# Sparse, dilated and windowed attention in one layer: choices of key blocks eight tiles apart, and the compression units' finishing cut in three

## The chip, the core and the metric

The kernel runs on one core of a Trainium2 chip. The engines are TensorE (PE for matmuls, PEld for weight loads), VectorE (DVE), ScalarE (ACT), GpSimd (POOL) and SyncE (SP, which issues transfers). The metric is the device time of one launch in microseconds (us); lower is better. Rows of the profile write L12 for line 12 of the kernel before.

## The reference, cut to what matters

One transformer layer over 2048 tokens of width 1024: a norm and an input projection, a mix of three attentions, an output projection, and a gated feed-forward block. The change lies in the first attention, which has six query heads in two groups of three. It compresses the keys, attends to the compressed ones, and uses those probabilities to choose eight blocks of 64 keys for each query:

```python
s = jnp.where(c_valid, s - slopes[:, :, None, None] * c_dist, -jnp.inf)
m = jnp.max(s, axis=-1, keepdims=True)
p = jnp.exp(s - jnp.where(jnp.isfinite(m), m, 0.0))
den = jnp.sum(p, axis=-1, keepdims=True)
p_cmp = p / jnp.where(den > 0, den, 1.0)
o_cmp = jnp.einsum('ngrtc,ncgd->ntgrd', p_cmp, vc.astype(jnp.float32))
imp = jnp.einsum('ngrtc,cs->ngts', p_cmp, jnp.asarray(block_overlap(nc, ns)))
...
score = jnp.where(valid, jnp.where(forced, jnp.inf, imp), -jnp.inf)
_, idx = lax.top_k(score, n_sel)
...
o = g[..., 0:1] * o_cmp + g[..., 1:2] * o_slc + g[..., 2:3] * o_win.astype(jnp.float32)
```

## The kernel before

Four parts follow each other: `project`, `compress`, `attend` and `mix_ffn`. The change is in `attend`, which runs from about 720 us to about 1570 us of the span.

`attend` works through 36 units (`attention_units`, L1431), each one head of one attention with 16 tiles of 128 queries. The first 18 are six times a "k" unit (compressed keys, one block of 127 keys for every tile) followed by two "b" units (dilated windows, folds 1, 4 and 16). Counted from 0, the k units are 0, 3, 6, 9, 12 and 15. Units 18 to 23 are "c", then "w" and "s" alternate; "s" is the attention to the chosen blocks.

All engines go through one loop over tiles, `for n in range(N + 7)`, each in its own fixed order:

- TensorE makes scores into `s_ps`, three banks (`scores`), transposes the exponentials into `t_ps` (`turn`), multiplies them with the values once for four tiles (`weigh_values`), and transposes the result back to queries in rows (`turn_out`, L1988) into `on_ps`, of which there is one. `turn_out(g)` waits until group g-1 has been finished (`out_done`).
- VectorE adds the bias to each score and takes the row minimum (`bias`, L2133), which also frees the score's bank; copies every other batch of transposed blocks out of `t_ps` (`take`, L2034); and finishes each group of four tiles (`finish`): it scales `on_ps` and writes it to `oh`.
- ScalarE takes the exponentials (`weigh`, L2045), copies the other batches, and copies the product out (`take_out`, L2053).

A group is four tiles. Its `turn_out` comes ten tiles after its first tile. A period below is the time from one `turn_out` to the next. In it TensorE issues four scores. In k units and fold 16 all four come at the tile with n % 4 == 0, two tiles after `turn_out`; in folds 1 and 4 they come in pairs.

The finishing of a k group is a chain of five or six small instructions of VectorE (L2158 to L2171): the denominator's maximum, its reciprocal, times the gate, the share of each key block (into `imp` for the first head of three, else into `shares` and then an add, L2169), and the scaled output (L2171). Only the first, the share and the output read `on_ps`; the output releases it.

A choice (`choose`) is made for four tiles of queries of one head group, eight in all: the add (L2201), the eight largest (L2206), their replacement (L2211), a compare (L2217). TensorE then transposes the mask (`turn_choice`, L1997) and one engine copies it out (L2027). The table `chosen_at` sets the tile at which this transpose stands, and counts the mask as a batch that takes its turn among the batches of the two copying engines.

Of the kernel before, what the change touches and what calls it, by code (L numbers as in the profile page):

```python
# [11 lines left out]
ALU = mybir.AluOpType  # L12
AX = mybir.AxisListType

P = 128
# [3 lines left out]
NT = T // P  # L19
HD = 64  # L20
# [1160 lines left out]
R = 3  # L1181
# [3 lines left out]
NS = 32  # L1185
# [290 lines left out]
def attend(nc, idt, z_parts, v_heads, gates, bias_b, bias_c, bias_s, bias_w, own_block, sinks, cmp_bias, pick_bias,  # L1476
# [4 lines left out]
    units = attention_units()  # L1481
    NU = len(units)
    N = NU * NT
    kind = [u.kind for u in units]
    heads = [(u.kind if u.kind in "bck" else "a", u.h) for u in units]
# [14 lines left out]
    chosen_at = {}  # L1500
    for g in range(G):
        last = heads.index(("k", g * R + R - 1))
        for q in range(4):
            chosen_at[(last + 1) * NT + 4 * q + 11] = (g, q)
# [23 lines left out]
    for b, batch in enumerate(batches):  # L1528
        batch["eng"] = b % 2
        counts[b % 2] += 1  # L1530
        batch["count"] = counts[b % 2]
        batch["close"] = batch["of"][-1][0]
# [69 lines left out]
    with ExitStack() as ctx:  # L1602
# [435 lines left out]
        def _(act):  # L2038
# [29 lines left out]
            for n in range(N + 7):  # L2068
# [13 lines left out]
                if n < N:  # L2082
                    take(act, 0, closing[n])
# [4 lines left out]
        def _(dve):  # L2088
# [50 lines left out]

            def finish(g):  # L2140
# [16 lines left out]
                elif unit.kind == "k":  # L2157
                    dve.tensor_scalar(coef[:].unsqueeze(2), on[:, :, HD:HD + 1], 1e-30, None, ALU.max).then_inc(chain, 1)  # L2158
                    dve.wait_ge(chain, at + 1)
                    dve.reciprocal(coef[:], coef[:]).then_inc(chain, 1)  # L2160
                    dve.wait_ge(chain, at + 2)
                    dve.tensor_tensor(gcoef[:].unsqueeze(2), coef[:].unsqueeze(2), gate[:, i:i + 4, 3 * unit.h:3 * unit.h + 1],
                                      ALU.mult).then_inc(chain, 1)
                    share = on_ps[:, :, HD + 1:HD + 1 + NS]
                    part = imp[:, i:i + 4, :] if unit.h % R == 0 else shares[:]
                    dve.tensor_tensor(part, share, coef[:].unsqueeze(2).to_broadcast([P, 4, NS]), ALU.mult).then_inc(chain, 1)
                    dve.wait_ge(chain, at + 4)
                    if unit.h % R:
                        dve.tensor_tensor(imp[:, i:i + 4, :], imp[:, i:i + 4, :], shares[:], ALU.add).then_inc(chain, 1)  # L2169
                        dve.wait_ge(chain, at + 5)  # L2170
                    dve.tensor_tensor(rows[:, :, 0:HD], on[:, :, 0:HD], gcoef[:].unsqueeze(2).to_broadcast([P, 4, HD]),  # L2171
                                      ALU.mult).then_inc(out_done, 1)
# [22 lines left out]
            def choose(g, q, stage):  # L2195
                tiles, count = slice(4 * q, 4 * q + 4), 4 * g + q
                if stage == 0:
                    dve.wait_ge(chain, links[4 * heads.index(("k", g * R + R - 1)) + 4])
                    if count == 0:
                        dve.wait_ge(pick_in, 16)  # L2200
                    dve.tensor_tensor(score[:, tiles], imp[:, tiles], pick[:, tiles], ALU.add).then_inc(score_done, 1)  # L2201
                    return
# [34 lines left out]
            for n in range(N + 7):  # L2237
                for stage in range(4):
                    if n + 4 - stage in chosen_at:
                        choose(*chosen_at[n + 4 - stage], stage)  # L2240
# [4 lines left out]
                if n < N:  # L2245
                    for piece, a, z in chunks(n):
                        if piece is not None:
                            bias(*piece)
                        take(dve, 1, closing_in(n, a, z))
                    take(dve, 1, [b for b in closing[n] if batches[b]["u"] is None])  # L2250
# [4 lines left out]
                if n >= 10 and (n - 10) % 4 == 0:  # L2255
                    finish((n - 10) // 4)

# [1148 lines left out]
```

## Time and profile before

| | |
|---|---|
| median of 3 runs | 3128.64 us (3128.58 to 3129.77) |
| profiled execution, its own time | 3130.43 us |
| its span | 3128.6 us |
| PE busy | 3037.5 us, 97% |
| PEld busy | 2480.4 us, 79% |
| DVE busy | 2057.8 us, 66% |
| ACT busy | 1472.6 us, 47% |
| POOL busy | 1201.7 us, 38% |
| mean granted TensorE clock | 0.995 |

Busy time of PE counts matmuls whose ends are modelled, so 97% does not say that it never waits. The shares are means over stages with different limits. The profiled execution's own time is 1.8 us above its span, and 1.8 us above the median of the runs.

### The profile page before, as it was taken

To read this page: it belongs to the slowest core of one execution; us is meant where nothing else is said; L and a number is where in the kernel's file an instruction comes from. 1 tells how busy PE (TensorE), PEld (TensorE's weight loads), DVE (VectorE), ACT (ScalarE), POOL (GpSimd) and SP (SyncE) were. 2 spreads that over 40 slices of the span, in tenths; PEclk is the share of its full clock that TensorE was granted. 3 is DMA by queue.
4 is the path that set the end of the run, shared out by engine and by line. 5 is a ranking of instruction groups with operands and counts; after the bars stand their busy time and mean duration, and the time that the engine had idled before them with its cause. 6 is when DMAs were issued, how large, how long until landed. Compare 5 with 4: busy or idle time off the path is not lost. (4 is left out here: it accounts for less than half of the span.)

```text
span 3128.6 us, 44854 instructions
## 1 busy us (share of the span) xinstructions
PE 3037.5 (97%) x16138; PEld 2480.4 (79%) x16138; DVE 2057.8 (66%) x3935; ACT 1472.6 (47%) x2656; POOL 1201.7 (38%) x840
## 2 busy tenths in 40 slices
PE   8999999999999999999999999999999999999998
PEld 8888888887777866667678778888888788888887
DVE  5565465556878977777744687777555577777343
ACT  5332443236777856666533544444334344444232
POOL 2444154310000034332110298888010688885010
PEclk9999999999999999999999999999999999999999
DMA  4464555366666622431244522222665222223553
GB/s 143 164 188 139 176 158 170 121 196 249 239 243 245 189 64 75 140 83 41 78 118 123 175 81 81 81 81 74 198 224 177 100 83 81 81 81 120 184 196 107
DMA packets 274811, 433.90 MB, mean 139 GB/s; under 512 B 125760, under 2 KB 178240, under 8 KB 261568
## 3 DMA queue, kind: packets, MB, share of 16 engines
q1 hardware_dynamic: 265600, 395.70, 38.5%
q0 software_dynamic: 8992, 35.33, 3.4%
q8 instruction: 131, 2.15, 0.3%
q14 instruction: 88, 0.72, 0.1%
HBM read 312.51 MB, written 126.84 MB: 140 GB/s over the span
## 5 line engine op out<-in xcount | busy, mean ns | idle before, releaser
L1111 PE MATMUL z_banks<-ops,z_area 128*128 128x512 f32 x1720 | 434.1, 391 | 3.2 <-DVE z_area L858 3.2
L3209 PE MATMUL f_banks<-f_wt 128*128 128x512 f32 x1776 | 406.1, 389 | 0.0
L3209 PEld LDWEIGHTS f_banks<-f_wt 128*128 128x128 f32 x1776 | 333.5, 188 | 69.0
L1111 PEld LDWEIGHTS z_banks<-ops,z_area 128*128 128x128 f32 x1720 | 323.3, 189 | 70.1 <-DVE z_area L858 3.6
L2579 POOL TENSOR_TENSOR f_wt<-f_wt_f,f_wt 128x1024 fp32r<-128x1024 f32 x132 | 316.2, 2418 | 64.6 <-ACT f_wt L2710 59.1
L2045 ACT ACTIVATE w_small<-w_small,a_stats 128x128 f32<-128x128 f32 (+3 forms) x510 | 256.7, 517 | 51.5 <-DVE a_stats L2133 38.2
L3180 PE MATMUL f_banks<-low,f_wt 128*128 128x512 f32 x704 | 274.2, 389 | 0.0
L3001 DVE SCALAR_TENSOR_TENSOR near<-w_small,vk,near 128x1024 f32<-128x1024 f32 x88 | 231.2, 2627 | 1.7
L1975 PE MATMUL a_ot_ps<-a_turned_w,vs 128*64 128x256 f32 (+3 forms) x1452 | 220.9, 427 | 0.0
L2133 DVE CUSTOM_DVE_ANT_0 w_small<-a_s_ps,near 128x128 f32<-128x128 f32 (+2 forms) x456 | 163.9, 391 | 85.2 <-PE a_s_ps L1931 74.0
L3180 PE MATMUL f_banks<-f_oo,f_wt 128*128 128x512 f32 x704 | 217.2, 390 | 2.4 <-ACT kc_f L2744 1.2
L1942 PE MATMUL a_t_ps<-idt,w_small 128*128 128x128 f32 x1092 | 211.6, 280 | 6.5 <-ACT w_small L2045 2.8
L2034 ACT ACTIVATE a_turned_w<-a_t_ps 128x512 f32<-128x512 f32 (+3 forms) x255 | 138.5, 548 | 154.7 <-PE a_t_ps L1942 154.4
L3001 DVE SCALAR_TENSOR_TENSOR w_small<-w_small,vk 128x1024 f32<-128x1024 f32 x88 | 158.1, 1796 | 66.5 <-ACT w_small L2770 66.5
L3012 DVE TENSOR_TENSOR f_wt<-f_wt_f,f_wt 128x512 fp32r<-128x512 f32 x88 | 60.8, 691 | 208.0 <-ACT f_wt L2783 207.8
L3145 PE MATMUL f_banks<-f_wt,f_oo 128*128 128x512 f32 x768 | 179.3, 392 | 1.3 <-DVE f_wt L2542 1.3
L1975 PEld LDWEIGHTS a_ot_ps<-a_turned_w,vs 128*64 128x64 f32 x1452 | 106.0, 136 | 93.1 <-issue 76.0
L2775 ACT ACTIVATE near<-near 128x1024 f32<-128x1024 f32 x44 | 46.8, 1063 | 268.0 <-DVE near L3001 268.0
L2780 ACT ACTIVATE f_wt<-f_wt_f 128x1024 fp32r<-128x1024 f32 x74 | 78.3, 1058 | 200.9 <-DMA f_wt_f<-in_w_ffn 200.7
L1111 PE MATMUL z_banks<-low,z_area 128*128 128x512 f32 x560 | 168.4, 391 | 1.4 <-DVE z_st_lo L923 1.4
L2034 DVE COPY a_turned_w<-a_t_ps 128x512 f32<-128x512 f32 (+3 forms) x251 | 157.1, 627 | 17.2 <-PE a_t_ps L1942 15.8
L3145 PEld LDWEIGHTS f_banks<-f_wt,f_oo 128*128 128x128 f32 x768 | 142.8, 188 | 31.4 <-DVE f_wt L2542 2.6
(307 smaller groups left out, 7068.1 us busy)
## 6 DMA issues: line engine op xcount, KB each, us to landing
low<-z_parts SPq DMA_DIRECT2D x46, 1024.0 KB, 6.1
f_wt_f<-in_w_ffn SPq DMA_DIRECT2D x74, 512.0 KB, 4.0
z_area_f<-in_w_z SPq DMA_DIRECT2D x54, 512.0 KB, 5.1
f_raw_f<-in_w_ffn SPq DMA_DIRECT2D x22, 1024.0 KB, 4.8
f_wt_f<-in_w_ffn SPq DMA_DIRECT2D x22, 1024.0 KB, 5.3
g_up<-near SPq DMA_DIRECT2D x44, 512.0 KB, 2.6
f_wt_f<-g_up SPq DMA_DIRECT2D x88, 256.0 KB, 4.3
z_parts<-z_st_hi SPq DMA_DIRECT2D x68, 256.0 KB, 2.3
```

The costliest lines, as they stand in the source:

```text
L1111: last = pe.matmul(banks[:, bank, :], w[:, c * P:(c + 1) * P], rows[:, c * 512:(c + 1) * 512], start=(first and c == 0 and q == 0), stop=( ...
L1942: ins = pe.transpose(t_ps[:, b % TB, i, :], weights(n)[:, x * P:(x + 1) * P], idt[:])
L1975: ins = pe.matmul(ot_ps[lines, at:at + count * P], values, rows, start=(x == mine[0]), stop=(x == mine[-1]), skip_group_check=True)
L2034: ins = eng.activation(out, src, ACT.Copy) if e == 0 else eng.tensor_copy(out, src)
L2045: act.activation(weights(n), weights(n), ACT.Exp, bias=negm[:, n % 32:n % 32 + 1], scale=-1.0, accum_out=total).then_inc(weighed, 1)
L2133: dve.tensor_tensor_reduce(weights(n)[:, a:z], s_ps[:, c % SB, 0:z - a], table[:, at + a:at + z], -0.125, floor, ALU.add, ALU.min, low).th ...
L2579: pool.tensor_tensor(a_lo(n, first, count), src, a_hi(n, first, count).bitcast(F32), ALU.subtract)\
L2780: act.activation(hi, raw, ACT.Copy).then_inc(wdh_done, 1)
L3001: dve.scalar_tensor_tensor(out=acc[b], in0=u[:, b, i:HALF + i], scalar=cw[:, b, i, j:j + 1], in1=acc[b], op0=ALU.mult, op1=ALU.add).then_i ...
L3145: last = pe.matmul(mix[:, k, n * 512:(n + 1) * 512], oo[:, k, part, c, :], w_part(w, c)[:, n, :], start=(c == 0 and i == 0), stop=(c == DC ...
L3180: last = pe.matmul(banks[:, 4 * (n % 2) + bank, :], w[:, c * P:(c + 1) * P], rows[:, c * 512:(c + 1) * 512], start=(first and c == 0 and x ...
L3209: last = pe.matmul(banks[:, 2 * t + n, :], g[:, tok], w[:, n, :], start=(d == 0 and x == 0), stop=(d == NF - 1 and x == 2))
```

## The change

1. `chosen_at` puts the eight mask transposes eight tiles apart (positions 3 and 11 of the two units behind the third and the sixth k unit) where they were four apart (positions 11, 15 of the first and 3, 7 of the second). The first one of each head group comes eight tiles earlier and the last one four tiles later. The four stages on VectorE come 6, 4, 3 and 2 tiles ahead of the transpose; they came 4, 3, 2 and 1 ahead. The first stage waits only for the group of tiles that it reads.
2. All eight masks are copied by ScalarE, one tile after their transpose and ahead of the batches of that tile. Before, the engines took turns: ScalarE had two and VectorE six. The other batches keep their turns by number.
3. `finish` of a k group becomes `finish_k` in three parts over three tiles: maximum and reciprocal at the old place; gate product and share at the end of the next tile; the add and the scaled output at the end of the tile after that.

```diff
-            chosen_at[(last + 1) * NT + 4 * q + 11] = (g, q)
+            chosen_at[(last + 1) * NT + 8 * q + 3] = (g, q)
...
-        batch["eng"] = b % 2
-        counts[b % 2] += 1
-        batch["count"] = counts[b % 2]
+        batch["eng"] = b % 2 if batch["u"] is not None else 0
+        counts[batch["eng"]] += 1
+        batch["count"] = counts[batch["eng"]]
...
-                    take(act, 0, closing[n])
+                    picks = [b for b in closing[max(n - 1, 0)] if batches[b]["u"] is None]
+                    take(act, 0, picks + [b for b in closing[n] if batches[b]["u"] is not None])
...
+            def finish_k(g, part):
+                u, on = g // 4, on_ps[:, :, 0:HD + 1]
+                unit, n, at = units[u], out_at.of_unit[u], links[g]
+                s, i = out_at.slot[n], 4 * (g % 4)
+                if part == 0:
+                    dve.wait_ge(out_turned, g + 1)
+                    dve.tensor_scalar(coef[:].unsqueeze(2), on[:, :, HD:HD + 1], 1e-30, None, ALU.max).then_inc(chain, 1)
+                    dve.wait_ge(chain, at + 1)
+                    dve.reciprocal(coef[:], coef[:]).then_inc(chain, 1)
+                    return
+                if part == 1:
+                    dve.wait_ge(chain, at + 2)
+                    dve.tensor_tensor(gcoef[:].unsqueeze(2), coef[:].unsqueeze(2), gate[:, i:i + 4, 3 * unit.h:3 * unit.h + 1],
+                                      ALU.mult).then_inc(chain, 1)
+                    share = on_ps[:, :, HD + 1:HD + 1 + NS]
+                    out = imp[:, i:i + 4, :] if unit.h % R == 0 else shares[:]
+                    dve.tensor_tensor(out, share, coef[:].unsqueeze(2).to_broadcast([P, 4, NS]), ALU.mult).then_inc(chain, 1)
+                    return
+                dve.wait_ge(chain, at + 4)
+                if unit.h % R:
+                    dve.tensor_tensor(imp[:, i:i + 4, :], imp[:, i:i + 4, :], shares[:], ALU.add).then_inc(chain, 1)
+                    dve.wait_ge(chain, at + 5)
+                if g % 4 == 0 and n >= 2:
+                    dve.wait_ge(stored[s], out_count[n - 2])
+                dve.tensor_tensor(oh[:, s, i:i + 4, 0:HD], on[:, :, 0:HD], gcoef[:].unsqueeze(2).to_broadcast([P, 4, HD]),
+                                  ALU.mult).then_inc(out_done, 1)
...
-                    dve.wait_ge(chain, links[4 * heads.index(("k", g * R + R - 1)) + 4])
+                    dve.wait_ge(chain, links[4 * heads.index(("k", g * R + R - 1)) + q + 1])
...
-                for stage in range(4):
-                    if n + 4 - stage in chosen_at:
-                        choose(*chosen_at[n + 4 - stage], stage)
+                for stage, ahead in enumerate((6, 4, 3, 2)):
+                    if n + ahead in chosen_at:
+                        choose(*chosen_at[n + ahead], stage)
...
-                if n >= 10 and (n - 10) % 4 == 0:
+                if n >= 10 and n % 4 == 2 and kind[(n - 10) // 16] != "k":
                     finish((n - 10) // 4)
+                for part in range(3):
+                    m = n - 10 - part
+                    if m >= 0 and m % 4 == 0 and kind[m // 16] == "k":
+                        finish_k(m // 4, part)
```

How the rows move on VectorE. First place: unit 6, first group. Before, from the gate product of its finishing on (L2162 gate product, L2166 share, L2169 add, L2171 output, L2133 biases, each with the read of its minimum):

```order
L2162 TENSOR_TENSOR a_gcoef<-a_coef,a_gate 128x4
L2166 TENSOR_TENSOR a_shares<-a_on_ps,a_coef 128x128
L2169 TENSOR_TENSOR a_turned_w<-a_turned_w,a_shares 128x128
L2171 TENSOR_TENSOR a_oh<-a_on_ps,a_gcoef 128x4x64
L2133 ISA w_small,a_stats<-a_s_ps,near 128x128
L2133 ISA a_stats 128x1
L2133 ISA w_small,a_stats<-a_s_ps,near 128x128
L2133 ISA a_stats 128x1
L2133 ISA w_small,a_stats<-a_s_ps,near 128x128
L2133 ISA a_stats 128x1
L2133 ISA w_small,a_stats<-a_s_ps,near 128x256
L2133 ISA a_stats 128x1
```

The same place of the changed kernel (L2153 gate product, L2157 share, L2134 biases, L2161 add, L2165 output):

```order
L2153 TENSOR_TENSOR a_gcoef<-a_coef,a_gate 128x4
L2157 TENSOR_TENSOR a_shares<-a_on_ps,a_coef 128x128
L2134 ISA w_small,a_stats<-a_s_ps,near 128x128
L2134 ISA a_stats 128x1
L2134 ISA w_small,a_stats<-a_s_ps,near 128x128
L2134 ISA a_stats 128x1
L2134 ISA w_small,a_stats<-a_s_ps,near 128x128
L2134 ISA a_stats 128x1
L2134 ISA w_small,a_stats<-a_s_ps,near 128x256
L2134 ISA a_stats 128x1
L2161 TENSOR_TENSOR a_turned_w<-a_turned_w,a_shares 128x128
L2165 TENSOR_TENSOR a_oh<-a_on_ps,a_gcoef 128x4x64
```

The add and the output have moved behind the four biases of the next scores.

Second place: a choice. Before, in unit 7 (L2206 the largest, L2211 replacement, L2217 compare, L2154 and L2156 the finishing of a b group):

```order
L2206 MAX a_turned_w<-a_turned_w 128x8 x4
L2133 ISA w_small,a_stats<-a_s_ps,near 128x128
L2133 ISA a_stats 128x1
L2133 ISA w_small,a_stats<-a_s_ps,near 128x256
L2133 ISA a_stats 128x1
L2211 MATCH_REPLACE a_turned_w<-a_turned_w 128x32 x4
L2217 TENSOR_SCALAR a_turned_w<-a_turned_w 128x128
L2154 COPY a_oh<-a_stats 128x4x2
L2156 TENSOR_REDUCE a_oh<-a_on_ps 128x4x64
```

In the changed kernel the first choice stands within unit 6, second group. It begins with the output of the group before (L2165), and L2213 is the choice's add, L2218 the largest, L2223 half of the replacement:

```order
L2165 TENSOR_TENSOR a_oh<-a_on_ps,a_gcoef 128x4x64
L2213 TENSOR_TENSOR a_turned_w<-a_turned_w 128x128
L2147 TENSOR_SCALAR a_coef<-a_on_ps 128x4
L2149 RECIPROCAL a_coef<-a_coef 128x4
L2218 MAX a_turned_w<-a_turned_w 128x8 x4
L2034 COPY a_turned_w<-a_t_ps 128x512
L2153 TENSOR_TENSOR a_gcoef<-a_coef,a_gate 128x4
L2157 TENSOR_TENSOR a_shares<-a_on_ps,a_coef 128x128
L2223 MATCH_REPLACE a_turned_w<-a_turned_w 128x32 x2
L2134 ISA w_small,a_stats<-a_s_ps,near 128x256
L2134 ISA a_stats 128x1
L2134 ISA w_small,a_stats<-a_s_ps,near 128x256
```

The first half of the replacement now stands ahead of the group's four biases, within a k unit, between the second and the third part of its finishing.

## Rows read from the trace of the kernel before

**Rows 1.** Windows, k units 0, 3, 6, 9, 12, 15: start:end, length, busy PE, PEld, DVE, ACT, POOL

```profile
734.10:750.18 16.08, 14.11 (x93) 11.02 (x92) 13.94 (x62) 11.19 (x36) 0.00 (x0) 0.89 0.22 79
776.83:790.80 13.97, 12.70 (x94) 9.90 (x92) 12.14 (x58) 11.05 (x36) 0.00 (x0) 1.00 0.37 125
817.61:831.71 14.10, 12.49 (x91) 9.67 (x89) 12.14 (x60) 10.81 (x36) 0.00 (x0) 1.00 0.31 108
863.53:876.95 13.42, 12.65 (x91) 9.68 (x90) 11.09 (x56) 10.78 (x36) 0.00 (x0) 1.00 0.39 135
904.76:918.34 13.58, 11.64 (x88) 8.60 (x87) 10.65 (x59) 9.29 (x35) 0.00 (x0) 1.00 0.36 122
946.49:960.64 14.15, 11.63 (x88) 8.59 (x87) 11.23 (x64) 9.29 (x35) 0.00 (x0) 1.00 0.33 113
```

**Rows 2.** Windows, same columns: unit 7 and unit 16 (choices), between them unit 10 (none)

```profile
831.71:850.12 18.41, 16.26 (x134) 13.04 (x133) 17.69 (x105) 12.57 (x44) 1.97 (x4) 1.00 0.77 273
876.95:891.35 14.40, 14.38 (x119) 11.72 (x118) 10.65 (x47) 12.33 (x42) 0.00 (x0) 1.00 0.86 320
960.64:977.72 17.08, 14.54 (x145) 12.09 (x145) 14.73 (x96) 10.95 (x42) 1.99 (x4) 1.00 0.75 286
```

**Rows 3.** Timeline of unit 6, first period: start, duration, engine, line, out<-in

```profile
817.61 0.50 PE L1988 MATMUL a_on_ps<-idt,a_ot 97*128 97x97 f32 x4
...
818.15 0.16 DVE L2158 TENSOR_SCALAR a_coef<-a_on_ps 128x4 f32<-128x4 f32 x1 [0.28 <-PE a_on_ps L1988]
...
818.64 0.28 DVE L2166 TENSOR_TENSOR a_shares<-a_on_ps,a_coef 128x128 f32<-128x128 f32 x1
...
818.84 0.31 PE L1930 MATMUL a_s_ps<-kc,low 128*128 128x128 f32 x1
...
818.96 0.29 DVE L2169 TENSOR_TENSOR a_turned_w<-a_turned_w,a_shares 128x128 f32<-128x128 f32 x1
...
819.29 0.42 DVE L2171 TENSOR_TENSOR a_oh<-a_on_ps,a_gcoef 128x256 f32<-128x256 f32 x1
...
819.63 0.28 DVE L2133 CUSTOM_DVE_ANT_0 w_small<-a_s_ps,near 128x128 f32<-128x128 f32 x1
...
819.97 0.39 PE L1930 MATMUL a_s_ps<-k_hi,low 128*128 128x256 f32 x1 [0.27 <-DVE a_stats L2133]
...
820.62 0.42 DVE L2133 CUSTOM_DVE_ANT_0 w_small<-a_s_ps,near 128x256 f32<-128x256 f32 x1 [0.28 <-PE a_s_ps L1931]
...
820.71 0.50 PE L1988 MATMUL a_on_ps<-idt,a_ot 97*128 97x97 f32 x4
```

**Rows 4.** Timeline of unit 6, second period

```profile
821.91 0.27 PE L1942 MATMUL a_t_ps<-idt,w_small 128*128 128x128 f32 x1
...
822.73 0.68 DVE L2034 COPY a_turned_w<-a_t_ps 128x512 f32<-128x512 f32 x1
...
823.32 0.42 DVE L2133 CUSTOM_DVE_ANT_0 w_small<-a_s_ps,near 128x256 f32<-128x256 f32 x1
...
823.80 0.39 PE L1930 MATMUL a_s_ps<-k_hi,low 128*128 128x256 f32 x1 [0.97 <-DVE a_stats L2133]
...
824.71 0.42 PE L1988 MATMUL a_on_ps<-idt,a_ot 97*128 97x97 f32 x3
```

**Rows 5.** Timeline of unit 6, third and fourth period: first score's end, fourth period's start

```profile
826.03 0.28 PE L1931 MATMUL a_s_ps<-k_lo,low 128*128 128x256 f32 x1
...
828.11 0.50 PE L1988 MATMUL a_on_ps<-idt,a_ot 97*128 97x97 f32 x4
...
829.78 0.28 PE L1931 MATMUL a_s_ps<-k_lo,low 128*128 128x256 f32 x1
```

**Rows 6.** Timeline of unit 7, VectorE: the parts of one choice

```profile
835.56 0.46 DVE L2206 MAX8 a_turned_w<-a_turned_w 128x8 f32<-128x32 f32 x4
...
836.48 0.08 DVE L2211 MATCH_VALUE_LOAD a_turned_w<-a_turned_w 128x8 f32 x1
...
837.25 0.23 DVE L2217 TENSOR_SCALAR a_turned_w<-a_turned_w 128x128 f32<-128x128 f32 x1
```

More of the change, by code:

```diff
@@ L2156, in finish @@
                     dve.tensor_reduce(rows[:, :, 0:HD], halves, AX.X, ALU.add).then_inc(out_done, 1)
[L2157 to L2172, printed above, removed]
                 elif unit.kind == "c":
@@ L2249, in _ @@
                         take(dve, 1, closing_in(n, a, z))
-                    take(dve, 1, [b for b in closing[n] if batches[b]["u"] is None])
                 if n == 7:
```

## The prediction

> **What bounds the kernel now.** I read the windows of the attention first, then the timeline of TensorE beside VectorE. The windows show the six k units at 13.4 to 16.1 us each, 85.3 us together, with VectorE busy for 10.7 to 13.9 us of each and TensorE for 11.6 to 14.1 [rows 1]. Neither is full: they wait for each other. Unit 7, which carries four choices, takes 18.41 us, and there VectorE is busy for 17.69 of it; unit 10, the same kind of unit without choices, takes 14.40, with TensorE busy for 14.38 and VectorE for 10.65. Unit 16 takes 17.08 with VectorE at 14.73 [rows 2]. So the choices are bound by VectorE, plain b units by TensorE, and only what happens in these eight or ten units can change; everything behind them is shifted by the sum, since TensorE goes through its program in one order and its waits behind the attention are not on the parts that the change touches.
>
> The timeline shows how a k period hangs together [rows 3]. Call T the start of `turn_out`. VectorE starts the finishing at T+0.54, needs 1.48 for its six instructions (818.15 to 819.63), and only then makes the first bias. The fourth score waits 0.27 for that bias, since there are three score banks. `turn_out` of the next group follows at T+3.10. In the second period a batch copy of 0.59 (822.73 to 823.32) lies between, the wait is 0.97, and the period is 4.00 [rows 4]. The change aims at these two waits and at unit 7.
>
> What is easily overlooked is the release of `on_ps`. The output of the finishing ends at 819.29+0.42 = 819.71, one microsecond before TensorE wants to overwrite it at 820.71 [rows 3]. That slack is the quantity to watch.
>
> **Part 1: the finishing in three.** Nothing is added to or taken from VectorE's instructions. The first part stays at T+0.54, the second (gate product and share, about 0.28 in all) comes a tile later, and the third, add and output, goes behind the biases of the tile with n % 4 == 0. In a k unit those are all four biases of the period, and the fourth needs the fourth score. TensorE has only three transposes between that score and the next `turn_out`, which waits for `out_done`. So a new chain closes in each period: `turn_out`, scores, four biases, add, output, `turn_out`. Its links by rows:
>
> - First period of unit 6. The first score starts at T+1.23 [rows 3]. A bias starts 0.65 after its 256-wide score (819.97 to 820.62), which I take as 0.59 for one of 128: T+1.82. That is no longer held up, as the first two parts are done by about T+1.3. The fourth score starts 0.34 later (819.63 to 819.97), T+2.16; its bias 0.65 later, T+2.81. The add starts 0.35 behind the start of this bias: an instruction of VectorE of 0.42 without a dependent one behind it is followed after 0.34 (819.29 to 819.63). That is T+3.16; the output 0.33 behind the add (818.96 to 819.29), T+3.49; it lasts 0.42, and TensorE restarts 0.06 after VectorE's end (823.32+0.42 to 823.80 [rows 4]): **3.97, now 3.10**.
> - Second period. The batch copy can start when the transposes of T+1.20 are done (821.91, 0.27 long [rows 4]), T+1.52. With 0.59 for the copy, 0.28 for the second part (the share's own length, overlapping with the gate product) and 0.32 for half a replacement (the first choice of its head group now stands here; four replacements take 836.48 to 837.25 [rows 6]) the first bias is at T+2.71, the fourth score 0.48 later (823.32 to 823.80), its bias 0.65, then 0.35, 0.33, 0.42 and 0.06: **5.00, now 4.00**.
> - Third. First score's end at T+1.60 (826.03+0.28 [rows 5]); the biases at 1.75 and 2.10, a copy of three blocks for 0.47 (estimate from the 0.59 for four), the second part 0.28, biases of 0.20 (0.28 less the same overlap) and 0.35, which brings the add to T+3.75: 3.75+0.33+0.42+0.06 = **4.56, now 3.40**.
> - Fourth. TensorE has the next unit's values first, so the first score ends at T+1.95 (829.78+0.28 less 828.11 [rows 5]), 0.35 later; no copy but 0.32 of replacement: **4.76, now 3.60**.
>
> Unit 6 so goes from 14.10 to 18.3, +4.2. The others by the same links, without the replacement except in unit 15: unit 3, where the pairs are all 256 wide, 3.97+4.68+4.71+4.8 = 18.2, +4.2. Unit 9 is the first head of three and has no add (0.33 less): 3.64+4.35+4.23+4.58 = 16.8, +3.4. Unit 12, before fold 16, has 128-wide blocks, 0.2 less a period: 3.77+4.36+3.77+4.6 = 16.5, +2.9. Unit 15 is the same with choices, and has one in its last period already (14.15 against unit 12's 13.58 [rows 1]): 16.6, +2.5. Unit 0 is like unit 9 with wider blocks, and the gates' arithmetic now stands ahead of the third part: at least unit 9's +3.4, I take +3.7. **Sum +20.9 us.** The two waits of rows 3 and 4 do go, but they were inside the present periods and are replaced by a longer one.
>
> Bounds: if VectorE's third part found its operands earlier than I chain it, or the fourth bias were not the last, the least is the saving of the two waits, 1.24 a unit, -7 us. If each release also delayed the next values by a further 0.3, it is +28. I take the chain, since all its links are neighbouring rows of these very instructions.
>
> The Trainium skill (page "Perfetto Trace Analysis", section on matmuls) says that independent groups of matmuls should rotate through PSUM banks, so that emptying one overlaps the next. It speaks against holding the one `on_ps` longer; with a second buffer the sum would be the -7 above instead of +20.9. No row here shows such a second buffer.
>
> **Part 2: choices eight apart.** One choice costs VectorE 0.46 for the largest, 0.77 for the replacements, 0.23 for the compare [rows 6] and about 0.28 for the add (as long as the share, equally 128 wide [rows 3]): 1.5 to 1.7. Two b groups without choice hold 2 x 2.7 of VectorE in 2 x 3.60 [rows 2]; with one choice that is 6.9 in 7.2, so TensorE bounds them. It has four mask transposes more in one of the two, about 0.4. Unit 7: 3.96+3.75+3.96+3.8 = 15.5 for 18.41, -2.9. Unit 16: 15.3 for 17.08, -1.8. The choices that moved into units 8 and 17 add 0.35 each; those in k units are in the sums above, where their other stages fit in VectorE's wait behind the output or behind the reciprocal. **Sum -4.0 us.** The second bound is 0: the choices gain nothing if ScalarE's copies delay its exponentials.
>
> **Part 3: the masks' copies.** Six copies of at most 0.68 (a copy of the same width [rows 4]) leave VectorE; they were in units 7 and 16 and are in the sum of part 2. ScalarE gets six more, in front of the batches of the next tile and what follows them. ScalarE is busy for 12.3 of 14.4 us in unit 10 [rows 2], so one copy fits but two in a group of batches are tight: up to +0.3 each, +2 in all, in the range. Masks are stored long before the "s" units read them; GpSimd's and SyncE's queues see the same transfers. SyncE's store of a k head waits up to 2 us longer, beside a slot that is free for a whole unit.
>
> **Sum:** +20.9-4.0 = +16.9, less 0.3 for the first period behind a k unit, where VectorE no longer catches up: **+16.6 us**. On the profiled execution's 3130.43 that is 3147.0; the median of the runs shown lies 1.8 lower, so I predict **3145.2**.
>
> **The rivals.**
> - *VectorE's work was the bound in k units, so half of the new wait replaces idle time.* For it: in units 3 and 6 VectorE is busy for 12.14 of about 14 us [rows 1]. Against it: unit 12 has 10.65 of 13.58 and the same chain. Then +10.5-4.0: 3135 to 3139. Chance 0.16.
> - *Faster: TensorE does not reach the release before the output is written.* This decides the sign: the third part must end within the time of the three transposes, 0.74 after the fourth score starts (819.97 to 820.71 [rows 3]); by the links it needs 0.65+0.35+0.42, and 0.33 for the add. If it did, the two waits vanish (-7) and the choices give -4.0: 3117.6. Chance 0.06.
> - *It cancels:* choices give twice what I take, by 17.69 of 18.41 busy in unit 7, and the wait a third: 3128 to 3134. Chance 0.06.
> - *The wait spreads:* ScalarE's mask copies and the late releases also hold the batches: 3149 to 3155. Chance 0.08.
> - *My chain as computed:* 3145.2, on its own 3140 to 3149. Chance 0.64.
>
> The rule of rotating banks adds no case of its own: its result is that of the second rival, were there a second buffer.
>
> **Numbers.** A measurement can tell about 0.2%, 6.3 us, from no change: the border lies at 3134.9. All of my own case, of the spreading wait and nearly all of the first rival lie above: slower 0.88; same 0.06; faster 0.06. The range 3135.5 to 3151 leaves out the two low rivals and the tail of the spreading one, under 2 in 10.
>
> **What would show it.** In the changed profile: each k unit 2.5 to 4.2 us longer; TensorE idle ahead of the output transposes by 0.5 to 1.2 in each k period, ended by VectorE's output; no wait of a fourth score in the first periods. Unit 7 near 15.5 with VectorE under 15 busy; unit 16 near 15.3. ScalarE with eight mask copies. I am wrong if the transposes into `on_ps` start without a wait, if k units stay near 14, or if the time is under 3135.

## The result, and the profile after

The changed kernel takes **3151.74 us** (median of 4 runs, 3149.41 to 3153.54) beside 3129.2 for the kernel before on the same chip (4 runs, 3128.58 to 3130.61): a ratio of 1.0072, 95% interval 1.006 to 1.0084. I forecast 3145.2 in a range of 3135.5 to 3151.0. Slower is right, and so is the mechanism below; the size was too small, +16.6 us forecast and +22.5 measured, and the median lies 0.7 us above the range. The two profiled executions are 3149.41 and 3130.43 us, +19.0. Three launches of 6000 to 9700 us, two of the kernel before beside the experiments and one of the version with the add late alone, are left out as slow ones.

Below are windows of the changed kernel, each from the first `turn_out` of a unit to the first of the next: start:end, length, then busy time of PE, PEld, DVE, ACT, POOL, the granted TensorE clock, DMA share, GB/s. The k units 0, 3, 6, 9, 12 and 15 come first, then units 7 and 16.

```profile
732.92:753.21 20.29, 14.87 (x94) 10.89 (x92) 13.79 (x64) 12.14 (x39) 0.00 (x0) 0.92 0.20 75
779.86:798.24 18.38, 13.40 (x93) 9.85 (x92) 12.80 (x62) 12.45 (x41) 0.00 (x0) 1.00 0.28 93
824.89:843.54 18.65, 13.77 (x95) 9.95 (x93) 14.63 (x88) 11.72 (x40) 0.58 (x1) 1.00 0.23 81
873.79:891.31 17.52, 13.37 (x91) 9.62 (x89) 10.96 (x57) 11.94 (x39) 0.00 (x0) 1.00 0.26 90
919.15:936.06 16.91, 12.49 (x88) 8.68 (x87) 10.78 (x60) 10.23 (x39) 0.00 (x0) 0.99 0.28 96
965.64:982.72 17.08, 13.08 (x92) 9.07 (x91) 12.62 (x85) 10.78 (x40) 0.50 (x1) 1.00 0.25 85
843.54:859.64 16.10, 15.21 (x124) 12.39 (x125) 14.00 (x76) 11.97 (x40) 1.00 (x2) 1.00 0.89 311
982.72:997.99 15.27, 13.99 (x136) 11.34 (x137) 11.67 (x72) 10.13 (x38) 0.99 (x2) 1.00 0.87 323
```

The six k units took 85.30 us [rows 1] and take 108.83. Unit 12 shows it best: VectorE is busy for 10.78 us as against 10.65, and yet the unit is 3.3 us longer. It isn't work that was added, but a wait. Units 7 and 16 took 18.41 and 17.08 [rows 2]. Over all 18 units of this part the time goes from 258.4 to 279.9 us; the 18 units behind them add 0.3, and the rest of the program is 2.8 shorter (1.2 of it ahead of the attention), which is within what two executions differ by.

What TensorE waits for between 725 and 1030 us, before and then after (us in total, times, longest):

```profile
PE a_s_ps L1930 <- DVE a_stats L2133: 17.2, 30, 1.5
PE a_t_ps L1942 <- ACT w_small L2045: 2.8, 8, 0.9
```

```profile
PE a_on_ps L1988 <- DVE a_oh L2165: 19.0, 24, 1.9
PE a_s_ps L1930 <- DVE a_stats L2134: 12.3, 21, 1.6
PE a_t_ps L1942 <- ACT w_small L2045: 3.0, 10, 0.5
```

The first line after is new, and its 24 times are the 24 groups of the six k units, all of them. The waits for a bias lost only 4.9 us. Nine of them are gone, in the first periods among others: that is what the change was to remove.

The chain in the first period of unit 6, TensorE and VectorE of the changed kernel (start, duration, engine, line, out<-in, idle before and its releaser). Its `turn_out` is T = 824.89:

```profile
824.89 0.50 PE L1988 MATMUL a_on_ps<-idt,a_ot 97*128 97x97 f32 x4
...
827.03 0.39 PE L1930 MATMUL a_s_ps<-k_hi,low 128*128 128x256 f32 x1
...
828.92 0.53 PE L1988 MATMUL a_on_ps<-idt,a_ot 97*128 97x97 f32 x4 [0.77 <-DVE a_oh L2165]
...
834.03 0.52 PE L1988 MATMUL a_on_ps<-idt,a_ot 97*128 97x97 f32 x4 [0.82 <-DVE a_oh L2165]
...
838.67 0.53 PE L1988 MATMUL a_on_ps<-idt,a_ot 97*128 97x97 f32 x4 [1.12 <-DVE a_oh L2165]
```

```profile
827.68 0.42 DVE L2134 CUSTOM_DVE_ANT_0 w_small<-a_s_ps,near 128x256 f32<-128x256 f32 x1 [0.23 <-PE a_s_ps L1931]
...
828.03 0.29 DVE L2161 TENSOR_TENSOR a_turned_w<-a_turned_w,a_shares 128x128 f32<-128x128 f32 x1
...
828.35 0.42 DVE L2165 TENSOR_TENSOR a_oh<-a_on_ps,a_gcoef 128x256 f32<-128x256 f32 x1
```

The fourth score starts at 827.03 with no wait, where it waited 0.27 before [rows 3]. Its bias follows at T+2.79, the add at T+3.14, the output at T+3.46. The output ends at 828.77, and 0.15 us later `turn_out` starts. The next three periods end in the same wait.

### The profile page after: what moved, and what is told of

It is laid out like the page before. It is cut to its first block and busy times, and to the rows that moved or that the text cites. A ratio compares the mean times of both kernels' runs of the same rounds, so it can differ in the third digit from the quotient of the medians.

```text
span 3147.6 us, 44857 instructions
## 1 busy us (share of the span) xinstructions
PE 3042.3 (97%) x16138; PEld 2479.2 (79%) x16138; DVE 2057.3 (65%) x3931; ACT 1475.5 (47%) x2660; POOL 1203.9 (38%) x840
## 5 line engine op out<-in xcount | busy, mean ns | idle before, releaser
L2134 DVE CUSTOM_DVE_ANT_0 w_small<-a_s_ps,near 128x128 f32<-128x128 f32 (+2 forms) x456 | 164.6, 392 | 98.3 <-PE a_s_ps L1931 85.4
```

The lines of the kernel that those rows point to most:

```text
L2134: dve.tensor_tensor_reduce(weights(n)[:, a:z], s_ps[:, c % SB, 0:z - a], table[:, at + a:at + z], -0.125, floor, ALU.add, ALU.min, low).th ...
```

## The experiments

The theory (release): the scaled output is the last reader of the one `on_ps`; issued two tiles later, it keeps TensorE from the next `turn_out`. The rivals: the choices and mask copies are what costs; three parts cost by themselves through VectorE's order. A fourth question came from the windows: TensorE's clock.

### The finishing in parts, alone

This is the kernel before with the last piece of the change's diff, its `finish_k` and the wait that goes with it; choices, their stages and the mask copies stay.

```diff
-                if n >= 10 and (n - 10) % 4 == 0:
+                if n >= 10 and n % 4 == 2 and kind[(n - 10) // 16] != "k":
                     finish((n - 10) // 4)
+                for part in range(3):
+                    m = n - 10 - part
+                    if m >= 0 and m % 4 == 0 and kind[m // 16] == "k":
+                        finish_k(m // 4, part)
```

> The kernel before with only the finishing of k units cut into three parts; choices and mask copies stay as before. Release theory (the scaled output, now issued two score tiles later, holds the one output bank, so the next turn of an output waits for VectorE): 20 to 24 us above before, near 3150 us, the six k units 17 to 20 us each, TensorE waiting 0.5 to 1.3 us for a_oh ahead of output transposes in them, units 7 and 16 as long as before (18.4 and 17.1). Theory that the moved choices and the mask copies on ScalarE are what costs: no more than 5 us above before.

Measured: 3158.09 us (3155.37 to 3161.39), ratio 1.0094, interval 1.0076 to 1.0112: +29 us, more than the whole change. TensorE's waits:

```profile
PE a_on_ps L1988 <- DVE a_oh L2164: 21.5, 24, 2.0
PE a_s_ps L1930 <- DVE a_stats L2133: 13.9, 22, 1.6
```

Unit 7 takes 18.44 as before, so the choices are not what lengthens. I had expected 20 to 24. In this execution the clock fell in units 0, 13 and 16, and the periods there are some 6.5 us longer than their like at the full clock: 6.75 and 5.95 us in unit 0 against 5.33 and 4.78, 4.78 and 4.91 in unit 13 against 3.60 and 3.57, 5.78 in unit 16 against 4.37. The rest, 24.2 of 30.7 over the 18 units, is 0.2 above what the theory says; unit 0's first period, at the lower clock here (5.09 us at 0.66) and in the kernel before (4.18 at 0.59), is part of it. Windows without the other engines (length, PE busy, clock, DMA share, GB/s):

```profile
744.81:751.56 6.75, 4.97 (x23) 0.75 0.00 0
751.56:757.51 5.95, 5.10 (x30) 0.71 0.00 0
990.21:995.99 5.78, 5.27 (x37) 0.70 0.49 108
```

### Choices and masks, alone

```diff
-                for part in range(3):
-                    m = n - 10 - part
-                    if m >= 0 and m % 4 == 0 and kind[m // 16] == "k":
-                        finish_k(m // 4, part)
+                elif n >= 10 and n % 4 == 2:
+                    for part in range(3):
+                        finish_k((n - 10) // 4, part)
```

> The kernel after with the finishing whole again in its old place; choices eight tiles apart and all mask copies on ScalarE stay. Release theory: 3125 to 3131 us, that is 20 to 26 us under after; TensorE has no wait for a_oh; units 7 and 16 near 16 and 15.3 us (before 18.4 and 17.1), with 1 to 3 us of it given back in the k units 6 and 15, where the last choices now stand. Theory that choices and masks cost: 3140 us or more.

Measured: 3130.2 us (3126.4 to 3133.19), ratio 1.0004, interval 0.9994 to 1.0013: no difference from before. There is no wait for `a_oh`. Units 6, 7 and 15 (columns as in the first windows):

```profile
817.26:832.93 15.67, 12.96 (x94) 10.09 (x93) 14.36 (x83) 11.06 (x37) 0.58 (x1) 1.00 0.30 103
832.93:849.00 16.07, 15.19 (x126) 12.37 (x125) 14.36 (x79) 12.57 (x44) 1.00 (x2) 1.00 0.84 306
946.47:961.44 14.97, 12.09 (x93) 8.99 (x92) 12.52 (x81) 10.24 (x37) 0.50 (x1) 1.00 0.30 104
```

Units 7, 8, 16 and 17 together go from 63.7 to 60.3 us. But unit 6 goes from 14.10 [rows 1] to 15.67, unit 9 from 13.42 to 13.77 and unit 15 from 14.15 to 14.97: 2.7 of the 3.3 come back. Unit 9 has no choice in it; its 0.35 comes with the mask copies, as a run below shows. In unit 6's second period VectorE holds the largest of the choice and two replacements (the last one is shown) ahead of the first bias:

```profile
822.03 0.43 DVE L2165 TENSOR_TENSOR a_oh<-a_on_ps,a_gcoef 128x256 f32<-128x256 f32 x1
822.37 0.46 DVE L2218 MAX8 a_turned_w<-a_turned_w 128x8 f32<-128x32 f32 x4
822.75 0.68 DVE L2034 COPY a_turned_w<-a_t_ps 128x512 f32<-128x512 f32 x1
...
823.57 0.18 DVE L2223 MATCH_REPLACE8 a_turned_w<-a_turned_w 128x32 f32<-128x32 f32 x1
823.66 0.42 DVE L2134 CUSTOM_DVE_ANT_0 w_small<-a_s_ps,near 128x256 f32<-128x256 f32 x1
```

In a k unit TensorE waits for the biases anyway, so what stands ahead of them there lengthens the period: this one takes 4.70 us, for 4.00 before.

### The output one tile earlier

```diff
+                    if g % 4 == 0 and n >= 2:
+                        dve.wait_ge(stored[s], out_count[n - 2])
+                    dve.wait_ge(chain, at + 3)
+                    dve.tensor_tensor(oh[:, s, i:i + 4, 0:HD], on[:, :, 0:HD], gcoef[:].unsqueeze(2).to_broadcast([P, 4, HD]),
+                                      ALU.mult).then_inc(out_done, 1)
                     return
-                dve.wait_ge(chain, at + 4)
                 if unit.h % R:
+                    dve.wait_ge(chain, at + 4)
                     dve.tensor_tensor(imp[:, i:i + 4, :], imp[:, i:i + 4, :], shares[:], ALU.add).then_inc(chain, 1)
-                    dve.wait_ge(chain, at + 5)
-                if g % 4 == 0 and n >= 2:
-                    dve.wait_ge(stored[s], out_count[n - 2])
-                dve.tensor_tensor(oh[:, s, i:i + 4, 0:HD], on[:, :, 0:HD], gcoef[:].unsqueeze(2).to_broadcast([P, 4, HD]),
-                                  ALU.mult).then_inc(out_done, 1)
```

> The kernel after with one instruction moved: the scaled output, whose end frees the output bank, goes from the third part of the finishing into the second, one score tile earlier; the third part keeps the addition of the shares alone. Release theory: nearly all of the loss goes, 3122 to 3132 us, with at most 0.2 us of wait for a_oh ahead of an output transpose. Theory that three separate parts cost by themselves (VectorE's order, whatever ends the release): no more than 5 us under after.

Measured: 3133.43 us (3131.38 to 3135.98), ratio 1.0014, interval 1.0005 to 1.0024. One instruction of 0.42 us, moved by a tile, takes back 18 of the 22 us. The waits in this run:

```profile
PE a_s_ps L1930 <- DVE a_stats L2134: 14.8, 21, 1.9
PE a_on_ps L1988 <- DVE a_oh L2161: 3.0, 7, 1.1
```

I had expected 0.2 us at the most, and 3.0 are left in 7 groups. Over the 18 units it stands 4.0 above the run of choices and masks alone, 261.8 against 257.8. About 1 of it is the lower clock in unit 0 (an estimate: its third period takes 6.02 us at 0.72, its second 4.98 at 1.00), and the rest is as much as these late releases.

### The third part within its tile, ahead of the biases

```diff
+                if n >= 12 and n % 4 == 0 and kind[(n - 12) // 16] == "k":
+                    finish_k((n - 12) // 4, 2)
...
-                for part in range(3):
+                for part in range(2):
```

> The kernel after with the third part (addition, scaled output) moved within its score tile: ahead of the two biases of that tile in place of behind them and their statistics. Release theory: the bank comes free earlier by about what two biases and the statistics take, some 1 to 2 us a period, which is as much as TensorE now waits for it (19.4 us in 24 waits): 3132 to 3142 us, a_oh waits under 10 us in all, part of it given back as later statistics (a_s_ps waits over 14 us). Theory that the parts themselves cost: 3149 us or more.

Measured: 3139.7 us (3137.61 to 3145.54), ratio 1.003, interval 1.0019 to 1.0042.

```profile
PE a_s_ps L1930 <- DVE a_stats L2134: 18.9, 27, 2.0
PE a_on_ps L1988 <- DVE a_oh L2165: 4.7, 7, 1.1
```

The wait for `a_oh` falls from 19.0 to 4.7, and the biases that now stand behind the output give 6.6 back. This and the run before it are one series: the earlier the output, the shorter the k units, 108.8, 97.4 and 92.2 us, and 88.1 with the finishing whole. The first three hold about 1 or 2 us at the lower clock each. The same instructions in the same three parts give all of them, so what costs is where the output stands, and not that there are parts.

### The changed kernel once more

This run has no edit.

> The kernel after unchanged, on the chip of the other three. All theories: 3149 to 3154 us. If the lower granted clock behind unit 12 is part of this kernel, a profile of it shows again a stretch behind a k unit at about half the clock, some 1.4 us in a period of 3.6; if it was one execution's chance, the clock is 1.00 there.

Measured: 3152.03 us (3151.18 to 3153.76). The k units of this profile are the same to 0.02 us in units 3, 6, 9 and 12, and the wait for `a_oh` is 19.4 us in 24. Behind unit 12 the clock is 1.00 this time, but it fell in unit 0's last period again, and in unit 15's third, which takes 5.97 us where the first profile had 4.29:

```profile
748.76:754.64 5.88, 5.10 (x30) 0.71 0.00 0
974.36:980.33 5.97, 5.08 (x22) 0.71 0.04 11
```

So the places differ from one execution to the next. What stays is that each profile of this kernel has two such stretches behind unit 0's first period, and that they cost 2.4 and 2.8 us. The repeat also has the lower clock in that first period, which takes 4.84 us at a mean clock of 0.76, for 3.86 at 1.00 in the first profile.

### Mask copies alone, and the places of the choices alone

Masks, in the kernel before:

```diff
-        batch["eng"] = b % 2
+        batch["eng"] = b % 2 if batch["u"] is not None else 0
...
-                    take(act, 0, closing[n])
+                    picks = [b for b in closing[max(n - 1, 0)] if batches[b]["u"] is None]
+                    take(act, 0, picks + [b for b in closing[n] if batches[b]["u"] is not None])
...
-                    take(dve, 1, [b for b in closing[n] if batches[b]["u"] is None])
```

Choices, in the kernel before, with the wait of the first stage that belongs to them:

```diff
-            chosen_at[(last + 1) * NT + 4 * q + 11] = (g, q)
+            chosen_at[(last + 1) * NT + 8 * q + 3] = (g, q)
...
-                for stage in range(4):
-                    if n + 4 - stage in chosen_at:
-                        choose(*chosen_at[n + 4 - stage], stage)
+                for stage, ahead in enumerate((6, 4, 3, 2)):
+                    if n + ahead in chosen_at:
+                        choose(*chosen_at[n + ahead], stage)
```

> The kernel before with the mask copies alone changed: all eight on ScalarE, one score tile later; choices and finishing as before. If VectorE's copies of masks are what lengthens the periods of units 7 and 16, these fall by 0.4 us in each period that had one, 3126 to 3129 us; if the places of the choices decide, units 7 and 16 stay at 18.4 and 17.1 us and the time is that of before within 1 us.

> Choices eight tiles apart, mask copies by turns on VectorE and ScalarE as before, finishing whole in its old place. Beside the run with choices and masks both changed (units 7 and 16 at 16.1 and 15.2 us, units 6, 9 and 15 longer by 2.7 us together, 0.6 us less over all 18 units): if the places of the choices carry it, units 7 and 16 come to within 0.5 us of these; if the masks on ScalarE carry it, they stay 1 us or more above. Time 3127 to 3132 us.

Measured: masks alone 3128.38 us (3125.09 to 3130.59), ratio 0.9997, interval 0.9987 to 1.0006; choices alone 3132.49 us (3129.56 to 3135.24), ratio 1.0008, interval 0.9999 to 1.0018. By the medians neither can be told from before; the traces say more. Masks alone take unit 7 to 16.83 and unit 16 to 16.26 us and leave the k units at 85.1, with unit 9 at 13.77 (0.35 longer, all in its last period) and unit 0 at 15.48, 0.6 shorter, as its first period is at the full clock here. The places alone take them to 17.16 and 15.51, but the k units to 89.5 (about 1 us of it in a stretch at the lower clock in unit 15), with unit 9 at 13.41 as before. So both parts carry the gain in units 7 and 16. The places carry what is given back in units 6 and 15, 2.4 us in the run with both, and the masks the 0.35 of unit 9. My either-or on unit 7 was wrong: it is 1.1 above the run with both, as the masks' theory had it, and unit 16 is within 0.3, as the other had it.

### More work for TensorE ahead of the wait

The first run has `FILL = 5`. The second has 15, and `if i < 3` in place of the last condition.

```diff
             def turn_out(g):
+                n = 4 * g + 10
+                if g and kind[(g - 1) // 4] == "k" and n < N:
+                    b, i = batch_of[n, units[n // NT].tiles[n % NT][-1]]
+                    if i == 2 and len(batches[b]["of"]) == 4:
+                        for _ in range(FILL):
+                            pe.transpose(t_ps[:, b % TB, 3, :], idt[:], idt[:])
```

> The kernel after with five more transposes of the identity on TensorE (their result is overwritten unread) in each key-compression period, right ahead of its wait for a_oh; nothing that is used is changed. Theory that the idle time there is what lets TensorE's clock fall behind k units: the granted clock is 1.00 in every period from unit 3 on, unit 0's last period 4.8 us in place of 5.8 to 5.9, unit 13's first 3.6; the periods otherwise as in the kernel after; the median 1 to 3 us under after (3149 to 3151) and its runs within 2 us. If the clock falls by chance, the median is that of after or above by what the transposes take.

> The kernel after with fifteen more transposes (in place of five) ahead of the wait for a_oh, and in the periods that had none, unit 0's last one among them; nothing that is used is changed. Theory that TensorE's idle time ahead of the output transposes is what lets the clock fall: 1.00 in every period behind unit 0's first, unit 0's last period near 4.8 us in place of 5.8 to 6.0, the median 1 to 3 us under after. Rival: the fillers hold TensorE where it no longer waits, or the clock falls anyway: 3151 us or more.

Measured: with five 3150.9 us (3149.37 to 3153.34), with fifteen 3165.54 us (3161.83 to 3169.37; ratio 1.012, interval 1.0103 to 1.0136). The five stand in 12 of the 24 k periods only. Unit 0's last period had none and again ran at a lower clock, 6.00 us at 0.72 (first row below). All others behind it are at 1.00, but the median is only 1.1 us under the repeat of the changed kernel, within the spread of both. Fifteen stand in every k period, and the first row of the second fence is unit 0's last period:

```profile
748.53:754.53 6.00, 5.10 (x30) 0.72 0.01 3
```

```profile
751.40:756.43 5.03, 5.03 (x45) 1.00 0.00 0
783.06:787.79 4.73, 4.61 (x35) 1.00 0.65 221
...
786.16 1.80 PE L1987 MATMUL a_t_ps<-idt 128*128 128x128 f32 x15
```

The clock then stays at 1.00 in every period behind unit 0's first, as the theory of the idle stretches says, in the one profile there is. They cost more than they save: fifteen take 1.80 us where the wait was about 0.8, and the rival was right on the time. The wait for `a_oh` is 0.3 us in this profile: it isn't shorter, the added work stands in its place.

### A version that beats both

In it, part 1 ends with the output and part 2 is the add alone, as in the run with the output one tile earlier. Parts 0 and 1 stand together in the old place. The other two versions have the same finishing, but the choices' places of the kernel before, one with all mask copies on ScalarE and one with these as before too.

```diff
-            chosen_at[(last + 1) * NT + 8 * q + 3] = (g, q)
+            chosen_at[(last + 1) * NT + 8 * q + (11, 7)[g]] = (g, q)
...
-                for part in range(3):
-                    m = n - 10 - part
-                    if m >= 0 and m % 4 == 0 and kind[m // 16] == "k":
-                        finish_k(m // 4, part)
+                elif n >= 10 and n % 4 == 2:
+                    finish_k((n - 10) // 4, 0)
+                    finish_k((n - 10) // 4, 1)
+                if n >= 12 and n % 4 == 0 and kind[(n - 12) // 16] == "k":
+                    finish_k((n - 12) // 4, 2)
```

> A version meant to beat both: the finishing of a k unit at once in its old place but in the order largest, reciprocal, gate product, share, scaled output; only the addition of the shares is put off, behind the biases two tiles later. Choices eight tiles apart, those of the first head group eight tiles later and of the second four tiles later than in the kernel after, masks on ScalarE. Release theory (the addition can go late because nothing waits for it, the output cannot): no a_oh wait, k units at or under those of the kernel before, 3118 to 3127 us. Theory that any finishing in parts costs in k units: 3130 us or more.

> The finishing as in the version meant to beat both (output at once, only the addition put off), with choices and masks as in the kernel before. Release theory: units 3, 6, 12 and 15, the ones with an addition, shorter by 0 to 0.3 us a period than in the kernel before, 3124 to 3128 us; units 7 and 16 unchanged. The other theory: 3130 us or more.

> The same finishing, and the mask copies all on ScalarE (alone these took units 7 and 16 from 18.4 and 17.1 to 16.8 and 16.3 us, 1.2 us of the median); choices as in the kernel before. If the two gains add: 3122 to 3127 us; if the choices eight tiles apart are needed for the rest of the gain, it is 1 us or more above the version with them.

| | median us | range | ratio, 95% interval | 18 units | k units |
|---|---|---|---|---|---|
| add late, masks, choices later | 3123.53 | 3120.58 to 3126.43 | 0.9982 (0.9974 to 0.9991) | 252.6 | 82.2 |
| add late alone | 3126.24 | 3123.81 to 3129.90 | 0.9992 (0.9983 to 1.0001) | 254.2 | 81.3 |
| add late, masks | 3124.91 | 3120.15 to 3129.17 | 0.9985 (0.9976 to 0.9993) | 253.3 | 82.4 |

All three medians fall where expected. The first and the third are somewhat under 0.2% faster than the kernel before, with 1 outside their intervals; the interval of the add late alone just holds 1. Units 6, 7 and 16 of the first, and its second period of unit 6 on VectorE:

```profile
814.89:828.17 13.28, 12.64 (x90) 9.67 (x89) 11.73 (x64) 10.77 (x36) 0.00 (x0) 1.00 0.33 116
828.17:844.25 16.08, 15.21 (x127) 12.38 (x126) 13.90 (x76) 12.58 (x44) 1.09 (x2) 1.00 0.84 298
954.23:969.48 15.25, 13.98 (x138) 11.32 (x138) 11.90 (x72) 10.78 (x42) 1.00 (x3) 1.00 0.87 324
```

```profile
819.22 0.41 DVE L2161 TENSOR_TENSOR a_oh<-a_on_ps,a_gcoef 128x256 f32<-128x256 f32 x1
819.55 0.68 DVE L2034 COPY a_turned_w<-a_t_ps 128x512 f32<-128x512 f32 x1
...
821.62 0.28 DVE L2166 TENSOR_TENSOR a_turned_w<-a_turned_w,a_shares 128x128 f32<-128x128 f32 x1
```

The output ends at 819.63, long before the next `turn_out` at 821.53; only the add, for which no engine waits, comes behind the biases. The gain is 5.8 us, from the same change of order as in the changed kernel, kept to the one instruction that can bear it. By the medians the late add has 3.1 of it, the masks 1.3 and the choices 1.4, but the intervals of neighbouring versions overlap, so these shares are not settled.

## Why the prediction was right in kind and short in size

- **The release as the new bound**: right. Unit 6's periods were forecast at 3.97, 5.00, 4.56 and 4.76 us and are 4.03, 5.11, 4.64 and 4.87. The links hold: fourth score at T+2.16 (is 2.14), its bias T+2.81 (2.79), add T+3.16 (3.14), output T+3.49 (3.46). The three runs that moved the output show it as cause.
- **The step that failed: "TensorE restarts 0.06 after VectorE's end".** That figure was read from a bias that releases a score bank [rows 4]. The output releases `on_ps` after 0.15 us, in each of the 24 groups between 0.14 and 0.16, and in the repeat too. Over 24 periods that is 2.2 us on a k sum of +20.9. The release of `on_ps` by the output ended no wait in the trace of the kernel before, so I took that of another operation and left its error out of the range; but 0.15 stood in that trace too, behind other waits (last section).
- **A second step that failed, a term put at nothing: the clock.** I counted every period at 1.00, though unit 0 had 0.89 in the kernel before [rows 1]. Unit 0's last period took 5.78 us where the like period of unit 3 took 4.78, and unit 13's first took 5.04 for 3.60: 2.4 us. In the repeat it was 2.8. With 2.2 for the links, +20.9 becomes 25.5 for the k units and unit 13, which measured +23.5 and +1.4. The 0.6 too much is what the kernel before lost itself in unit 0's first period: 4.18 us at 0.59, for 3.57 at 1.00 in the run with the masks alone.
- **Choices, -4.0**: units 7, 8, 16 and 17 give -3.3 (16.10 and 15.27 for the forecast 15.5 and 15.3; unit 8 rose by 0.74 for 0.35). That stages in k units "fit in VectorE's wait" was not so when the finishing is whole: they cost 2.4 us there, in units 6 and 15. With the late output unit 6 is 0.35 over the forecast, which is what its four releases make. **-0.3** behind k units: between -0.17 and +0.03 in units 4 and 10.
- **Added up** for the mean of the two profiles of the changed kernel: 280.65-258.4 = +22.3 over the 18 units. Forecast +16.6, and 2.2 for the releases, 2.6 for the clock, 0.7 for the choices and 0.2 for the last term make +22.3, beside +22.5 of the medians. That it fits so closely is in part luck: the 0.6 that the kernel before lost, 0.5 for the repeat's first period (half of 1.0) and the 0.35 of unit 9 are not in it and nearly cancel. The first profile was the fastest run of the four.
- **The rivals**: VectorE's work replacing idle time, a release in time and a cancellation all fail on the 24 waits. The spreading wait is the right time (3149 to 3155) for the wrong reason: the waits for ScalarE's exponentials went from 2.8 to 3.0 us only.
- **Rotating banks**: the rule of the Trainium skill (page "Perfetto Trace Analysis", section on matmuls) has the direction that the runs show: freeing the bank sooner is worth up to 22 us here (3151.7 against 3130.2 with the finishing whole). A second `on_ps` wasn't tried.

## What to carry to other kernels

Before a chain is split so that something else can go first, mark in it the instruction whose end releases a buffer, and measure how long before its next writer it ends; that slack (1.0 us here) is all that may be spent. Move only what nobody waits for: here one add. And take the release time from a wait that has the same rows in the waiting engine's program, or put both values in the range, when it is paid 24 times.

## What the runs showed of the hardware

**The time of a release goes with a separate wait row in TensorE's program.** It is 0.15 us from the end of the output on VectorE (128x256) to TensorE's transposes, and 0.06 from a bias to the next score. VectorE ended 1004 of TensorE's waits in the 14 profiles. In 320 of them a wait row of TensorE (EVENT_SEMAPHORE) stands between the end of VectorE's instruction and the next weight load, and the matmul starts 0.145 to 0.147 us after that end. In 670 there is no such row, and it starts after 0.053 to 0.057. In 14 there are two, and it is 0.26. VectorE's operation doesn't decide it: its copies out of `t_ps` have the row in 8 of 14 cases in the kernel before, and 0.15 in these eight, 0.06 in the others. In the code `turn_out` waits for two counts, `ot_taken` and `out_done`, and nearly every score for one. First, the wait rows of `out_done` in the kernel before between 725 and 1030 us (count, shortest, median and longest in ns, first and last start). Next, the one row ahead of the `turn_out` at 828.92 in the changed kernel. Last, two rows of the kernel before from which 0.15 could have been read (2207.25 + 0.68 = 2207.93, then 2208.08).

```profile
L1985 PEldq EVENT_SEMAPHORE  x82: 51/51/51, 737.7 to 1027.1; - x82
```

```profile
L1985 PEldq EVENT_SEMAPHORE  x1: 51/51/51, 828.8 to 828.8; - x1
```

```profile
2207.25 0.68 DVE L2964 TENSOR_TENSOR w_small<-f_banks,kc_f 128x512 f32<-128x512 f32 x1
...
2208.08 0.70 PE L3180 MATMUL f_banks<-f_xt,f_wt 128*128 128x512 f32 x2 [0.27 <-DVE w_small L2964]
```

No run has a `turn_out` with a single wait, so that the row is the cause is not shown.

**TensorE's clock fell behind short waits, in the middle of busy work.** One-microsecond windows of the changed kernel in unit 0, from the 1.9 us wait for `a_oh` on, which ends at 747.43 (length, PE busy, clock, DMA share, GB/s):

```profile
746.00:747.00 1.00, 0.00 (x0) 1.00 0.00 0
748.00:749.00 1.00, 1.00 (x7) 0.50 0.00 0
752.00:753.00 1.00, 0.53 (x5) 1.00 0.00 0
```

After the wait, with TensorE fully busy, the clock is 0.50 (1.2 of 2.4 GHz) for between three and four microseconds, then it is back. Behind unit 12, where the wait is 0.83 us, it is the same (the first period of unit 13, its mean clock 0.69):

```profile
936.06:941.10 5.04, 4.79 (x33) 0.69 0.53 115
```

A stretch costs 1.0 to 1.7 us beside the like period at 1.00. Within the 18 units, of the seven profiles of kernels without a wait for `a_oh` and without added transposes, six have no period at a lower clock behind unit 0's first and one has one. The six with that wait and without the fifteen transposes have one to five such periods. So the waits of some 1 us make it likelier. Unit 0's last period, behind a wait of 1.8 to 1.9 us, is at the lower clock in all four profiles that have that wait (the changed kernel, its repeat, the finishing in parts alone, five transposes). Which other period is hit differs between executions of the same kernel, and one profile each does not settle the rule.
